# Head-pair attention reordered: two units transposed together, the next two scored, the first two mixed

## The chip, the cores and the metric

The kernel runs on one core of one Trainium2 chip. The metric is the device time of one launch in microseconds (us). A matmul or a transpose runs on TensorE (PE in the profile; PEld is its weight load), maxima and multiplications on VectorE (DVE), exponentials and copies on ScalarE (ACT), small elementwise work on GpSimd (POOL), and SyncE (SP) issues the weight DMAs.

## The reference

The whole network is five blocks on 512 latent and 256 context tokens: one hybrid layer (a recurrent branch beside a latent attention, "MLA"), then four layers of the kinds A, B, C, A. The change touches one kind of attention, which occurs three times: the MLA branch (8 heads, query and key width 96, value width 64), and the two A layers, layer 0 and layer 3 (16 query heads on 4 key/value heads, width 64). All in float32.

```
def softmax_attend(q, k, v):                       # MLA: 512 queries, 768 keys
    s = jnp.einsum('bqhd,bkhd->bhqk', q, k).astype(jnp.float32) * ATTN_SCALE
    p = jax.nn.softmax(s, axis=-1).astype(v.dtype)
    return jnp.einsum('bhqk,bkhd->bqhd', p, v)
...
mla_l = o * jax.nn.silu(g_mla)

def gqa_attention(q, k, v):                        # A layers
    ...
        logits = jnp.einsum("bqhgd,bkhd->bhgqk", qb, k).astype(jnp.float32) * scale
        p = jax.nn.softmax(logits, axis=-1).astype(v.dtype)
        return jnp.einsum("bhgqk,bkhd->bqhgd", p, v)
...
    o = gqa_attention(q, concat([kc, k]), concat([vc, v]))      # 512 queries, 768 keys
    oc = gqa_attention(qc, kc, vc) if need_ctx else None         # 256 queries, 256 keys
...
x = x + gt * ((o * jax.nn.silu(z)) @ w_out)
```

Layer 0 needs the context output `oc` too, layer 3 does not.

## The kernel before, in words

`pair_attention` (line 1193) is written once for all three places. A *unit* is one tile of 128 queries of a pair of heads (m = 0 and 1). MLA has 16 units (4 head pairs, 4 query tiles), layer 3 has 32, layer 0 has 32 and then 8 "joined" units, in which the two context tiles of a head pair stand side by side with 256 keys each. Four units (in the joined part one) make a *group*, whose result is gated and stored at once.

The steps of a unit, with their lines:

- scores (L1342 for the A layers, L1350 for MLA, L1317 joined): q times k into PSUM, 128 x 768 for each head. The two 64-row heads of an A layer run beside each other in the array.
- maximum (L1542; L1536 joined) on DVE, exponential with a running sum (L1477; L1491 joined) on ACT, into `prob`. In the profile an exponential is followed by a read of the accumulator, and it is this read that frees those who wait for the sum or the exponentials.
- turn (L1377; L1360 joined): 12 PE transposes of 128 x 128, in groups of four that fill one PSUM bank.
- evictions of the turned banks into `prob_t`: ACT (L1499) takes two of the three, DVE (L1560) one.
- mix (L1402; L1387 joined): `prob_t` times v into the OUT bank.
- DVE takes the reciprocal of the sums (L1554), POOL multiplies the gate tile z by it (L1614; L1610 joined), PE transposes z (L1424; L1416 joined), ACT copies it to `gate_t` (L1463, L1484), DVE multiplies OUT by it (L1571, L1567).

PE runs its instructions in the order in which the Python loops write them: turn unit i, mix unit i-1, score unit i+2. The PSUM places of the scores rotate: `place(i, m)` gives each head of a unit two of the six banks 0 to 5, so three heads' scores fit at a time, and the score of a unit waits until an older unit's exponentials are done. Transposes go into the banks that their own unit's scores leave free, and into bank 6 (TURN). Bank 7 is OUT.

Beside the attention, six steps of the next layer's modulation are done in MLA and in layer 0: `sum_rows` (L379) multiplies a weight chunk by a wide silu vector on PE, `mod_take` (L396, L398) adds the result on DVE, and at the end `mod_columns` (L389) turns it. They use what is free of the banks beside the scores. `mod_operands` (L362 to L365, DVE) prepares the silu vector.

In the A layers the attention starts inside the projection stage that precedes it: unit 0 is scored before the last pair of projections, and two gate multiplications of that stage (L1076) and two tanh copies (L850) are still to be done when unit 1 is scored.

Of the kernel before, what the change touches and what calls it, by code (L numbers as in the profile page):

```python
# [22 lines left out]
P = 128  # L23
# [1153 lines left out]
def pair_units(pairs):  # L1177

    units, groups = [], []
    for pair in pairs:
        if pair.get("joined"):
            units.append(dict(group=len(groups), col=0, last=True, joined=True, tiles=pair["tiles"]))
        else:
            for u, tile in enumerate(pair["tiles"]):
                units.append(dict(group=len(groups), col=u, last=u == len(pair["tiles"]) - 1, joined=False, **tile))
        groups.append(dict(dst=pair["dst"], last=len(units) - 1, z=[t["z"] for t in pair["tiles"]]))
    return units, groups  # L1190


def pair_attention(pr, local, pairs, next_mod, spare=None, entry=None):
# [7 lines left out]

    (scored, maxed, exped, filled, taken_a, taken_v, summed, scaled, mixed, finished, operands) = (
        pr.counter(s) for s in (
            "at_scored", "at_maxed", "at_exped", "at_turned", "at_moved_a", "at_moved_v", "at_chained", "at_weighted",
            "at_mixed", "at_stored", "mod_operands"))
    units, groups = pair_units(pairs)
    n = len(units)
    single = sum(not u["joined"] for u in units)
    TURN, OUT = pr.bank(6), pr.bank(7)
    gate_out, columns_out = pr.counter("sub_gated"), pr.counter("mod_copied")  # L1210
    mod_rows_at = {}
    for c in range(6 if next_mod else 0):
        at = (c + 1) * single // 7
        mod_rows_at[at - 1 if units[at]["last"] else at] = c
    late_gates = {i + 1: u["group"] for i, u in enumerate(units) if u["last"] and single < n and i >= single - 1}
    gates_at = {i + 2: u["group"] for i, u in enumerate(units) if u["last"] and i + 1 not in late_gates}
    rows_at = {i + 2: c for i, c in mod_rows_at.items()}
    row_steps = sorted(rows_at)
    mod_cols_at = max(mod_rows_at, default=-4) + 1

    def joined(i):
        return i < n and units[i]["joined"]

    def kts(i):
        return 4 if joined(i) else units[i]["keys"] // P

    def parts(i):

        return kts(i) // 2

    filled_at, taken_at, in_turn = {}, {}, []
    for i in range(n):
        for g in range(parts(i)):
            filled_at[i, g] = len(filled_at) + 1
            on_v = g == 1
            taken_at[i, g] = (taken_v if on_v else taken_a), sum(1 for _, h in taken_at if (h == 1) == on_v) + 1
            if g == 2 or parts(i) == 1:
                in_turn.append((i, g))

    def taken(i, g):  # L1240
        by, count = taken_at[i, g]
        return by.at(count)

    if spare is None:
        prob = local("prob", [P, 3, 2, TOK])
        prob_t = entry.free[:, 0:24 * P].rearrange("p (u x q) -> p u x q", u=2, x=12)
    else:
        flat = pr.h_t[:, :, :].rearrange("p k t -> p (k t)")
        prob = flat[:, 0:6 * TOK].rearrange("p (u m k) -> p u m k", u=3, m=2)
        prob_t = spare[:, 0:24 * P].rearrange("p (u x q) -> p u x q", u=2, x=12)  # L1250
# [8 lines left out]
    def place(i, m):  # L1259

        return 2 * ((2 * i + m) % 3)

    def score(i, m, a=0, b=TOK):

        return pr.bank(place(i, m), 2)[:, a:b]

    def joined_bank(i, m):

        return pr.bank(2 * ((2 * single - 3 + i - single) % 3) + m)

    def late_bank(i, gate):

        if i == single - 1:
            return TURN if gate else OUT
        return pr.bank(6 + (i - single) % 2)[:, CTX * gate:CTX * gate + CTX]  # L1280

    def late_gate_t(i):

        half = 0 if i == single - 1 else CTX * ((i - single) % 2)
        return gate_t[:, half:half + (SEQ if i == single - 1 else CTX)]

    def beside(i, m):

        return pr.bank(place(i, m), 2)[:, TOK:TOK + 256]

    def turn_bank(i, g):

        if joined(i):
            return joined_bank(i, g)
        return TURN if g == 2 or parts(i) == 1 else pr.bank(place(i, 1) + g)

    def gate_part(group, m):

        half = P * len(groups[group]["z"]) // 2
        return slice(half * m, half * m + half)

    def halves(x):
        return x.rearrange("p (x q) -> p x q", q=P)

    def tensor(pe, part):
        def joined_score(i):
            if i == single + 1:
                pe.wait_ge(*exped.at(2 * single - 1))  # L1310
            else:
                before = single - 2 if i == single else single - 1 if i == single + 2 else i - 3
                for g in range(2):
                    pe.wait_ge(*taken(before, g))
            for t, tile in enumerate(units[i]["tiles"]):
                for m in range(2):
                    last = pe.matmul(joined_bank(i, m)[:, CTX * t:CTX * t + CTX], tile["q"][m], tile["k"][m],  # L1317
                                     start=True, stop=True)
                    if t:
                        last.then_inc(*scored.tick())  # L1320

        def do_score(i):
            if joined(i):
                joined_score(i)
                return
# [3471 lines left out]
```

## Time and profile before

| | us |
|---|---|
| median of 3 runs | 2799.93 |
| lowest, highest run | 2796.51, 2800.12 |
| span of the profiled execution | 2795.5 |
| attention of MLA, first turn to last store | 99.2 |
| attention of layer 0 | 184.6 |
| attention of layer 3 | 145.6 |

The profile comes from a separate execution and gives its span, from the first to the last instruction; no whole time is listed for that execution. The median of the timed runs is 4.4 us above its span. The three attention parts are 429.4 us of the span. In the timeline a line is a run of like instructions of one engine: start, length to the end of the last one, and in brackets the idle time before it and who ended it. The length counts the pipeline of the last matmul, so the distance from one run's start to the next one's is the time that PE spent on it.

### The profile page before, as it was taken

The numbers are of one execution on the slowest core, as the hardware profiler recorded it, in microseconds if no ns is written. First come the engines' busy times: TensorE is split into PE (matmuls) and PEld (weight loads), VectorE is DVE, ScalarE is ACT, GpSimd is POOL, SyncE is SP. The second block draws the span as 40 slices with busy tenths as digits, with TensorE's granted clock in tenths as the row PEclk, the third lists the DMA queues.
The fourth block names the chain that finished last, engine by engine and source line by source line (L and its number), as shares of the span: only waits on it lengthen the run. The fifth ranks groups of instructions, "written<-read, shape, count | busy, mean of one in ns | idle before, by whom it ended". The sixth has DMA issues, their size and how long they took to land. (4 is left out here: it accounts for less than half of the span.)

```text
span 2795.5 us, 57678 instructions
## 1 busy us (share of the span) xinstructions
PE 2690.8 (96%) x23772; PEld 2129.5 (76%) x23772; DVE 1702.0 (61%) x3049; ACT 954.5 (34%) x2216; POOL 834.6 (30%) x1067
## 2 busy tenths in 40 slices
PE   7999999999999999999999999999999899999998
PEld 5978788785745887767688867777888676868886
DVE  5667876864426836564753357659833777576665
ACT  2022323224422136642121248321212675222661
POOL 3323333240024510012323115236531444254000
PEclk9999999999999999999999999999999999999999
DMA  6230100112432113303011161131011311212100
GB/s 242 92 128 20 44 18 3 49 36 69 144 114 80 61 48 134 107 1 106 33 60 61 61 223 30 52 112 61 31 61 61 136 62 61 94 59 81 77 2 31
DMA packets 108422, 205.88 MB, mean 74 GB/s; under 512 B 21923, under 2 KB 26162, under 8 KB 107648
## 3 DMA queue, kind: packets, MB, share of 16 engines
q1 hardware_dynamic: 107888, 201.30, 20.6%
q8 instruction: 189, 3.10, 0.5%
q0 software_dynamic: 272, 0.89, 0.1%
q14 instruction: 73, 0.60, 0.1%
HBM read 186.85 MB, written 15.54 MB: 72 GB/s over the span
## 5 line engine op out<-in xcount | busy, mean ns | idle before, releaser
L739 PE MATMUL psum<-weights,h_t 128*128 128x256 f32 x1488 | 355.5, 382 | 5.5 <-ACT early_work L828 5.5
L739 PEld LDWEIGHTS psum<-weights,h_t 128*128 128x128 f32 x1488 | 281.0, 191 | 45.4 <-ACT early_work L828 6.7
L1542 DVE TENSOR_REDUCE neg_max<-psum 128x1 f32<-128x768 f32 x160 | 152.3, 953 | 67.5 <-PE psum L1342 47.4
L739 PE MATMUL psum<-z_l,x_tiles 128*128 128x256 f32 x816 | 192.8, 379 | 0.5 <-POOL z_l L954 0.5
L739 PEld LDWEIGHTS psum<-z_l,x_tiles 128*128 128x128 f32 x816 | 155.0, 190 | 21.9 <-issue 0.9
L839 ACT ACTIVATE early_work<-psum 128x512 f32<-128x512 f32 (+1 forms) x80 | 45.0, 565 | 365.4 <-DVE psum L1112 250.0
L1112 DVE TENSOR_TENSOR psum<-psum,early_work 128x512 f32<-128x512 f32 x62 | 43.1, 695 | 144.5 <-PE psum L739 144.5
L1614 POOL TENSOR_TENSOR z_l<-z_l,inv_total 128x128 f32<-128x128 f32 x64 | 25.6, 400 | 346.8 <-DVE inv_total L1554 291.2
L1477 ACT ACTIVATE prob<-psum,neg_max 128x768 f32<-128x768 f32 x128 | 115.7, 904 | 14.1 <-DVE neg_max L1542 9.2
L739 PE MATMUL psum<-weights,x_tiles 128*128 128x256 f32 x496 | 117.2, 379 | 0.0
L1499 ACT ACTIVATE early_work<-psum 128x512 f32<-128x512 f32 x136 | 81.5, 599 | 96.4 <-PE psum L1377 96.4
L790 PE MATMUL psum<-weights,h_t 128*128 128x512 f32 x256 | 111.5, 593 | 1.2 <-PEq L240 1.2
L739 PE MATMUL psum<-z_l,h_t 128*128 128x256 f32 x408 | 97.5, 382 | 7.4 <-DVE early_work L1099 7.4
L739 PEld LDWEIGHTS psum<-weights,x_tiles 128*128 128x128 f32 x496 | 94.2, 190 | 12.8
L2824 POOL TENSOR_TENSOR x_tiles<-x_tiles,delta 128x512 f32<-128x512 f32 x36 | 47.8, 1329 | 182.2 <-DVE delta L2743 181.7
L1342 PE MATMUL psum<-k_l,q_l 64*128 64x256 f32 x768 | 100.2, 393 | 1.5 <-ACT prob L1477 1.5
L1377 PEld LDWEIGHTS psum<-eye,prob 128*128 128x128 f32 x768 | 82.7, 141 | 22.1 <-issue 14.6
L1377 PE MATMUL psum<-eye,prob 128*128 128x128 f32 x768 | 98.1, 277 | 0.8 <-ACT prob L1477 0.8
L1402 PE MATMUL psum<-early_work,v_l 128*64 128x128 f32 x1536 | 98.0, 277 | 0.0
L790 PEld LDWEIGHTS psum<-weights,h_t 128*128 128x128 f32 x256 | 48.0, 190 | 61.8 <-issue 61.8
L739 PEld LDWEIGHTS psum<-z_l,h_t 128*128 128x128 f32 x408 | 77.2, 191 | 21.1 <-DVE early_work L1099 10.6
L1402 PEld LDWEIGHTS psum<-early_work,v_l 128*64 128x64 f32 x1536 | 82.5, 137 | 10.7 <-ACT early_work L1499 8.1
(534 smaller groups left out, 6456.9 us busy)
## 6 DMA issues: line engine op xcount, KB each, us to landing
weights<-in_ada_w_dram SPq DMA_DIRECT2D x30, 2048.0 KB, 8.1
weights<-in_a_w_in_dram SPq DMA_DIRECT2D x10, 2048.0 KB, 8.4
weights<-in_b_w_in_dram SPq DMA_DIRECT2D x8, 2048.0 KB, 7.8
weights<-in_c_w_in_dram SPq DMA_DIRECT2D x8, 2048.0 KB, 7.9
weights<-in_w_in_dram SPq DMA_DIRECT2D x6, 2048.0 KB, 8.8
x_aside<-x_tiles SPq DMA_DIRECT2D x24, 512.0 KB, 2.7
x_tiles<-x_aside SPq DMA_DIRECT2D x4, 3072.0 KB, 15.8
weights<-in_a_w_out_dram SPq DMA_DIRECT2D x4, 2048.0 KB, 7.9
```

The costliest lines, as they stand in the source:

```text
L739: last = pe.matmul(dst, lhs[:, k, :], rhs[k // 2][:, k % 2, :], start=k == 0, stop=k == KH - 1)
L790: last = pe.matmul(ps(i), pr.h_t[:, k, P * t:P * t + P], w[:, k, :], start=(k == 0), stop=(k == KT - 1))
L839: act.activation(square[:, j % 2, 0:w], ps(i)[:, 0:w], ACT.Square).then_inc(*squared.tick())
L1112: dve.tensor_tensor(left_ps, left_ps, terms[:, 0:2, :], ALU.add).then_inc(*projected.tick())
L1342: last = pe.matmul(score(i, m, a, a + 256), units[i]["q"][m], units[i]["k"][m][:, a:a + 256], start=True, stop=True)
L1377: last = pe.transpose(turn_bank(i, g)[:, P * x:P * x + P], prob[:, i % 3, m, P * kt:P * kt + P], pr.eye[:, :])
L1402: last = pe.matmul(OUT[64 * m:64 * m + 64, P * col:P * col + P], units[i]["v"][m][kt], prob_t[:, i % 2, 2 * kt + m, :], start=(kt == 0), s ...
L1477: act.activation(prob[:, i % 3, m, 0:keys], score(i, m, 0, keys), ACT.Exp, bias=neg_max[:, i % 4, m:m + 1], accum_out=total[:, i % 4, m:m ...
L1499: act.activation(prob_t[:, i % 2, 4 * g:4 * g + 4, :], halves(turn_bank(i, g)), ACT.Copy)\
L1542: last = dve.tensor_reduce(neg_max[:, i % 4, m:m + 1], score(i, m, 0, keys), AX, ALU.max, negate=True)
L1614: pool.tensor_tensor(z, z, wide(inv[:, i % 4, 0:2], 2, 64), ALU.mult).then_inc(*scaled.tick())
L2824: pool.tensor_tensor(pr.X[:, tiles[i], cols], pr.X[:, tiles[i], cols], delta[:, u % 2, :], ALU.add)\
```

## The change

`pair_attention` is rewritten around pairs of units (p, with units 2p and 2p+1); the arithmetic stays. In words:

- PE order: turn both units of pair p (24 transposes), score both units of pair p+1, then the row sums if there are any, then mix both units of pair p.
- PSUM: banks 0 to 2 belong to head 0, banks 3 to 5 to head 1. Each three banks hold the scores of the two units end to end (2 x 768 columns). The transposes of the pair go into the same banks, in three steps of eight: step e fills bank e (evicted by ACT) and bank 3+e (evicted by DVE), so each of the two has 1.5 evictions per unit. The scores of the next pair wait for those evictions step by step. Bank 6 (SIDE) serves gates, row sums and modulation columns; bank 7 is OUT.
- Step 0 waits for the exponentials of unit 2p, step 1 for those of unit 2p+1. The maximum of the second unit waits for the exponential of the first unit's same head, since the two share a bank.
- The gate transposes of a group stand before the last step of turns of its last pair, and wait there for POOL's multiplication (`scaled`). One ACT copy of 512 columns takes them.
- Joined units are also done in pairs: 4 pairs, four context tiles per group.
- Row sums after the scores of pairs 2, 4, ..., 12 (layer 0) or 0 to 5 (MLA), in one 512-column piece.
- At the start of an A layer unit 0 and unit 1 are scored where they were; pair 1 is scored after both are turned.

```
         if part == "first":
             if entry:
                 entry.scores(pe)
-            do_score(0)
+                score_alone(0)
+            else:
+                score_pair(0)
             return
         if entry:
             entry.second_place(pe)
-        for i in range(-1, n + 1):
-            if 0 <= i < n:
-                do_turn(i)
...
-            if i >= 1:
-                do_mix(i - 1)
...
-            if i + 2 < n or i + 2 in gates_at:
-                do_score(i + 2)
+            pe.wait_ge(*exped.at(2))
+            score_alone(1)
+        for p in range(n_pairs):
+            turn_pair(p)
+            if p + 1 < n_pairs:
+                score_pair(p + 1)
+            if p == 0 and entry:
+                entry.all_places(pe)
+            if p in rows_at:
+                sum_rows(p)
+            do_mix(2 * p)
+            do_mix(2 * p + 1)
+            if p == columns_at:
...
+                mod_columns(pe, SIDE[:, 0:48], mod_rows, pick).then_inc(*columns_done.tick())
```
```
+        def score_pair(p):
+            c, d = 2 * p, 2 * p + 1
...
+            if p:
+                wait_taken(p - 1, 0)
+            if by_rows:
+                for a in (0, 256):
                     for m in range(2):
+                        score(c, m, a, a + 256)
...
+            if p:
+                wait_taken(p - 1, 1)
             for m in range(2):
+                score(c, m, 512, 768)
+            for m in range(2):
+                score(d, m, 0, 256).then_inc(*scored.tick())
+            if p:
+                wait_taken(p - 1, 2)
+            if by_rows:
+                for m in range(2):
+                    score(d, m, 256, 512)
+                for m in range(2):
+                    score(d, m, 512, 768).then_inc(*scored.tick())
...
+        def turn_pair(p):
+            a, b = 2 * p, 2 * p + 1
...
+            def wait_gates():
+                pe.wait_ge(*scaled.at(b + 1))
+                if gates_at[p]:
+                    pe.wait_ge(*gate_out.at(gates_at[p]))
+                side_free(p)
+
+            pe.wait_ge(*exped.at(2 * a + 2))
+            for x, block in enumerate(blocks):
+                e, half, at = x // 8, x // 4 % 2, P * (x % 4)
+                if x == 8:
+                    pe.wait_ge(*exped.at(2 * b + 2))
+                if x == len(blocks) - 8 and zs:
+                    wait_gates()
+                    for y, z in enumerate(zs):
+                        pe.transpose(SIDE[:, P * y:P * y + P], z, pr.eye[:, :])
+                last = pe.transpose(half_place(half)[:, SEQ * e + at:SEQ * e + at + P], block, pr.eye[:, :])
+                if x % 8 == 7:
+                    last.then_inc(*filled.tick())
```
ScalarE and VectorE, their loops:
```
+        for p in range(n_pairs):                      # scalar
...
+            for e in range(steps(p)):
+                take_step(p, e)
+            if p in gates_at:
+                take_gate(gates_at[p])
+            if p + 1 < n_pairs:
+                for i in (2 * p + 2, 2 * p + 3):
+                    for m in range(2):
+                        do_exp(i, m)
...
+            if i % 2:                                 # vector, do_max
+                dve.wait_ge(*exped.at(2 * i + m - 1))
...
+        for p in range(n_pairs):                      # vector
+            if p - 1 in gates_at:
+                finish(gates_at[p - 1])
+            if p:
+                do_inverse(2 * p)
+                do_inverse(2 * p + 1)
+            for e in range(steps(p)):
+                take_step(p, e)
+            if p + 1 < n_pairs:
+                for i in (2 * p + 2, 2 * p + 3):
+                    for m in range(2):
+                        do_max(i, m)
+            if p == 0:
+                if beside_second:
+                    beside_second()
+                if next_mod:
+                    mod_operands(pr, dve, silu_w, pick, 1, operands, 6)
+                do_inverse(0)
+                do_inverse(1)
+            if p in rows_at:
+                c = rows_at[p]
+                dve.wait_ge(*rows_done.at(c + 1))
+                mod_take(dve, mod_rows[:, :], SIDE, c, rows_taken.at(max(c, 1))).then_inc(*rows_taken.tick())
+        finish(len(groups) - 1)
```

## Rows read from the trace of the kernel before

**Rows 1.** The page: span of the profiled execution.
```profile
span 2795.5 us, 57678 instructions
```
**Rows 2.** By stretch: busy PE, PEld, DVE, ACT, POOL; granted clock; DMA.
```profile
677.49:776.71 99.22, 97.66 (x905) 70.73 (x903) 47.11 (x79) 47.79 (x101) 6.01 (x15) 1.00 0.37 128
1045.00:1229.56 184.56, 182.22 (x1954) 142.82 (x1952) 112.71 (x190) 119.84 (x286) 18.89 (x48) 1.00 0.27 98
2591.55:2737.18 145.63, 143.36 (x1546) 118.39 (x1544) 90.37 (x135) 97.50 (x206) 12.77 (x32) 1.00 0.09 38
```
**Rows 3.** Timeline, layer 3: start, length, engine, line, [idle before].
```profile
2657.52 1.57 PE L1342 MATMUL psum<-k_l,q_l 64*128 64x256 f32 x12
2658.34 0.17 DVE L1554 RECIPROCAL inv_total<-total 128x2 f32<-128x2 f32 x1 [1.06 <-ACT prob L1477]
2658.59 0.40 POOL L1614 TENSOR_TENSOR z_l<-z_l,inv_total 128x128 f32<-128x128 f32 x1 [4.02 <-DVE inv_total L1554]
2659.02 1.53 PE L1377 MATMUL psum<-eye,prob 128*128 128x128 f32 x12
2660.15 0.69 DVE L1560 COPY early_work<-psum 128x512 f32<-128x512 f32 x1
2660.48 1.53 PE L1402 MATMUL psum<-early_work,v_l 128*64 128x128 f32 x24
2661.94 0.66 PE L1424 MATMUL psum<-eye,z_l 128*128 128x128 f32 x4
2662.53 1.57 PE L1342 MATMUL psum<-k_l,q_l 64*128 64x256 f32 x12
```
**Rows 4.** Timeline, start of layer 3: maxima and exponentials back to back.
```profile
2583.67 1.81 DVE L1542 TENSOR_REDUCE neg_max<-psum 128x1 f32<-128x768 f32 x2
2584.65 0.90 ACT L1477 ACTIVATE prob<-psum,neg_max 128x768 f32<-128x768 f32 x1 [4.46 <-DVE neg_max L1542]
2585.40 1.28 DVE L1076 SCALAR_TENSOR_TENSOR z_l<-tanh_z,z_l 128x512 f32<-128x512 f32 x2
2585.54 0.89 ACT L1477 ACTIVATE prob<-psum,neg_max 128x768 f32<-128x768 f32 x1
2586.32 0.20 ACT L1477 ACTIVATION_READ_ACCUMULATOR prob<-psum,neg_max 128x1 f32 x1
```
**Rows 5.** Timeline, layer 3, unit 1 after the first turn begins.
```profile
2591.65 0.96 DVE L1542 TENSOR_REDUCE neg_max<-psum 128x1 f32<-128x768 f32 x1 [0.27 <-PE psum L1342]
```
**Rows 6.** Timeline, layer 3's last turn, for which PE waits.
```profile
2731.16 0.19 ACT L1477 ACTIVATION_READ_ACCUMULATOR prob<-psum,neg_max 128x1 f32 x1
2731.40 1.53 PE L1377 MATMUL psum<-eye,prob 128*128 128x128 f32 x12 [0.77 <-ACT prob L1477]
```
**Rows 7.** Timeline, layer 0, a row sum and the scores behind it.
```profile
1065.62 1.93 PE L379 MATMUL psum<-weights,silu_wide 128*32 128x256 f32 x32
1067.48 1.57 PE L1342 MATMUL psum<-k_l,q_l 64*128 64x256 f32 x12
```
**Rows 8.** Timeline, layer 0's joined units.
```profile
1214.31 1.14 PE L1317 MATMUL psum<-k_l,q_l 64*128 64x256 f32 x8
1215.48 1.29 DVE L1536 TENSOR_REDUCE neg_max<-psum 128x2 f32<-128x512 f32 x2 [1.04 <-PE psum L1317]
1216.62 1.08 PE L1387 MATMUL psum<-early_work,v_l 128*64 128x256 f32 x8
1216.93 0.76 POOL L1610 TENSOR_TENSOR z_l<-z_l,inv_total 128x128 f32<-128x128 f32 x2 [2.56 <-DVE inv_total L1554]
```
**Rows 9.** Timeline, MLA: the turns of two neighbouring units.
```profile
682.36 1.48 PE L1377 MATMUL psum<-eye,h_t 128*128 128x128 f32 x12
687.91 1.48 PE L1377 MATMUL psum<-eye,h_t 128*128 128x128 f32 x12
```
**Rows 10.** By stretch, outside the attention (columns as in rows 2).
```profile
541.50:543.70 2.20, 1.56 (x50) 1.42 (x50) 2.17 (x4) 0.60 (x1) 0.00 (x0) 1.00 0.44 102
543.00:550.00 7.00, 5.13 (x116) 4.99 (x116) 4.88 (x8) 0.00 (x0) 2.44 (x3) 0.76 0.38 141
```

More of the change, by code:

```diff
@@ L1205, in pair_attention @@
             "at_mixed", "at_stored", "mod_operands"))
+    gate_out, columns_out = pr.counter("sub_gated"), pr.counter("mod_copied")
+    rows_done, rows_taken, columns_done = pr.counter("mod_multiplied"), pr.counter("mod_taken"), pr.counter("mod_turned")
     units, groups = pair_units(pairs)
[L1207 to L1238, printed above, removed]
@@ new lines, in joined, with half_place, score_at, blocks_of @@
+    def joined(i):
+        return units[i]["joined"]
+    def half_place(m):
+        return pr.bank(3 * m, 3)
+    def score_at(i, m):
+        if entry and i == 0 and m:
+            return pr.bank(2, 2)[:, 0:TOK]
+        size = SEQ if joined(i) else TOK
+        return half_place(m)[:, size * (i % 2):size * (i % 2) + size]
+    def blocks_of(i):
+        if joined(i):
+            return [(m, CTX * t + P * kt) for m in range(2) for kt in range(2) for t in range(2)]
+        return [(m, P * kt) for kt in range(units[i]["keys"] // P) for m in range(2)]
@@ new lines, in score_alone, with side_free @@
+        def score_alone(i):
+            for a in (0, 256, 512):
+                for m in range(2):
+                    last = score(i, m, a, a + 256)
+                    if a == 512:
+                        last.then_inc(*scored.tick())
+        def side_free(p):
+            before = [c for at, c in rows_at.items() if at < p]
+            if before:
+                pe.wait_ge(*rows_taken.at(max(before) + 1))
+            if 0 <= columns_at < p:
+                pe.wait_ge(*columns_out.at(1))
@@ new lines, in do_mix @@
+        def do_mix(i):
+            unit = units[i]
+            wait_taken(i // 2, steps(i // 2) - 1 if i % 2 else steps(i // 2) - 2)
+            if unit["at"] == 0 and unit["group"]:
+                pe.wait_ge(*finished.at(unit["group"]))
+            if joined(i):
+                for kt in range(2):
+                    for m in range(2):
+                        x = turned_at(i, 4 * m + 2 * kt)
+                        last = pe.matmul(OUT[64 * m:64 * m + 64, unit["at"]:unit["at"] + CTX], unit["tiles"][0]["v"][m][kt],
+                                         prob_t[:, x:x + 2, :].rearrange("p x q -> p (x q)"), start=(kt == 0), stop=(kt == 1))
+                last.then_inc(*mixed.tick())
+                return
+            kts = unit["keys"] // P
+            for kt in range(kts):
@@ L1385, in joined_mix @@
                 for m in range(2):
[L1386 to L1388 removed]
+                    last = pe.matmul(OUT[64 * m:64 * m + 64, unit["at"]:unit["at"] + P], unit["v"][m][kt],
+                                     prob_t[:, turned_at(i, 2 * kt + m), :], start=(kt == 0), stop=(kt == kts - 1))
@@ L1506, in scalar @@
             return
[L1507 to L1521 removed]
+        do_exp(1, 0)
```

380 lines of the change are left out of this document (116 added, 264 removed).

## The prediction

> **What bounds the kernel now.** I read the busy time of the three attention stretches first. PE is busy for 97.66 of 99.22, 182.22 of 184.56 and 143.36 of 145.63 us, DVE and ACT for 47 to 67% of it, at a full clock (1.00, the level of 2.4 GHz) [rows 2]. So PE's instruction stream sets the time, and every other engine has slack. The timeline then gives the period. In layer 3 a unit is scores at 2657.52, turns at 2659.02, mix at 2660.48, next kind at 2661.94: 1.50 + 1.46 + 1.46 = 4.42 us, with DVE's maximum, evictions and POOL's scaling beside it. A gate adds 0.59 (2661.94 to 2662.53) every fourth unit [rows 3]. Two pairs with one gate are 18.27 us, or 9.13 per pair.
>
> What part of a run is work and what is switching? Four transposes are 0.66 long and twelve 1.53 [rows 3]: 0.109 per transpose. Eight score records are 1.14 long and twelve 1.57 [rows 8, 3]: 0.217 per two heads' records, which run beside each other. Mix records come two at a time as well, twelve steps, again 0.109 each, since the run of 24 has the length of twelve transposes [rows 3]. So 1.46 for twelve steps of 0.109 = 1.31 leaves 0.15 for the change of kind; scores leave 1.50 - 1.30 = 0.20.
>
> **The change part by part.** The matmuls, transposes and columns are the same. What changes is the number of changes of kind and the waits.
>
> *PE's own work per pair of units* (A layers): turns 1.46 + 12 x 0.109 = 2.77, scores 1.50 + 6 x 0.217 = 2.80, mixes 2.77: 8.34 instead of 8.84. Half of the switching is gone, 0.50 us per pair. A gate inside the turns costs 4 x 0.109 = 0.44 instead of 0.59.
>
> *The new chain.* Before, three heads' scores are kept in rotation and the turns of a unit find their exponentials done two units ahead. Now six banks hold just one pair: nothing of pair p+1 can be scored before pair p is turned, and its exponentials must be done before its own turns. In that time PE has only the mixes. From S, the first score of a pair: the first unit's scores are signalled by the 8th step, 1.57 + 2 x 0.217 = 2.00. Two maxima back to back take 1.81 [rows 4] and one takes 0.96 [rows 5]; an exponential takes 0.98 to the end of its read (2585.54 to 2586.52), and the next may start 0.89 after it [rows 4]; a released engine starts about 0.04 later (PE at 2731.40 after a read that ended at 2731.35: 0.05) [rows 6].
>   - maxima c0, c1: 2.03 to 3.84, c0 done at 2.98. Exponentials c0: 3.02 to 4.00, c1: 3.91 to 4.90. The first unit is ready at 4.90.
>   - maximum d0 waits for exponential c0, 4.04 to 5.00; d1 for c1, 4.94 to 5.89. Exponentials d0: 5.04, d1: 5.93 to 6.92. The second unit is ready at 6.92, and PE may go on at 6.97.
>   - PE meanwhile: scores to 2.80, mixes to 5.57, the first eight transposes (ready at 4.90, no wait) to 6.45. Then it waits 0.52 until 6.97. The other 16 take 1.46 + 0.44 = 1.90: 8.87.
>
> So a pair takes 8.87, with its share of the gate (0.22) 9.09, against 9.13: the 0.50 won by fewer changes goes into a stall of 0.52 at the ninth transpose. The evictions do not prolong it: step 1 is filled at about 8.0, step 2 at 8.9, each eviction is 0.69 at most [rows 3], and the scores that need step 2 come 1.8 after the next S. That ACT has one half eviction less per unit is worth nothing, since ACT is not late anywhere.
>
> *Row sums* (L379) cost 1.86 each on PE (1065.62 to 1067.48) [rows 7]. In layer 0 they now stand ahead of the mixes, so they push the first transposes from 5.57 to 7.43, behind the point 6.97: of 1.86 only 1.86 - 0.52 = 1.34 lengthen the pair. Six of them: -3.1 us; the modulation columns the same way: -0.5.
>
> *Layer 3 in full.* First turn at 2591.55 [rows 2]. Unit 1: maximum at 2591.65, the second ends at 2593.46 (1.81), its exponential at 2594.5 [rows 4, 5]; PE's eight transposes are done at 2592.5 and it waits until 2594.57, then 1.90: S of pair 1 is 4.92 after the start. Then 15 x 8.87 = 133.05 and 8 gates x 0.44 = 3.5. Once, at pair 1, the gate transposes wait for POOL: DVE does the two held-over gate products (1.28 [rows 4]) after the maxima, and only then the four reciprocals, and POOL needs 4 x 0.40 [rows 3] behind them: PE is held about 1.2. Then mixes 1.53 + 1.31 = 2.84 and the last product 0.73 (0.69 for a 512-column DVE operation, as an eviction, and the release). Sum 146.2 against 145.63 [rows 2]: +0.6.
>
> *Layer 0.* The same 4.92 + 133.05 + 3.5, POOL's wait 1.6 (the modulation operands stand in DVE's way as well), row sums 6 x 1.34 = 8.0, columns 0.5: 151.6. Joined pairs: scores signalled at 1.13 and 1.99, maxima 1.29 for two [rows 8], eight exponentials of 256 columns; I take 0.46 for each, the rate at which half the width would go (0.89 / 2), and 0.1 for the last read, which puts the first unit at 3.8 and the second at 5.65. PE has scores and mixes until 3.8 and eight transposes until 4.8. The gate now stands at the ninth transpose and waits for DVE's reciprocal and POOL's two multiplications (0.76) [rows 8] behind the last exponential: 5.65 + 0.17 for the reciprocal [rows 3] + 0.76 + three releases of 0.05 = 6.74. Then 12 transposes, 1.46: 8.20 per joined pair, three times, 8.6 the first time (POOL is later there, behind a longer mix), and 2.7 for the end: 35.9. Together 187.5 against 184.56 [rows 2]: +2.9. This is the dearest piece, a wait of some 2 us four times.
>
> *MLA.* The unit is 5.55 (682.36 to 687.91) [rows 9], since the 96-row scores of the two heads do not run side by side. PE's stream per pair is then about 10.8, longer than the chain (second unit ready near 8.2), so there is no stall and the switching is won, with this array shape some 0.3 per pair: 7 x -0.3 = -2.2. Against it the first row sum, now behind pair 0, waits for the silu operands, which DVE makes after pair 1's four maxima: about +2.3. Row sums gain nothing here. Sum +0.1.
>
> Total: +0.6 + 2.9 + 0.1 = +3.6. The profiled span would be 2795.5 + 3.6 = 2799.1 [rows 1]; with the 4.4 us by which the median stands above the span, **2803.5 us**.
>
> Bounds. The stall per pair is the one number that counts, 24 to 31 times. From below: all of it gone, 0.52 x 30 = -16 us. From above: if releases and the paired DVE and ACT work each run a tenth late (seven links), 0.4 more per pair, +12. The joined wait lies between nothing (-8) and a whole unit's chain, 3.8 more once per pair (+15); I take the value worked out, whose links all have rows.
>
> **A rule against the change.** In the nearest place of this trace a stretch of transposes alone (541.5 to 543.7) still has the granted clock 1.00, and in the 7 us after it, with PE busy for 5.13, the mean falls to 0.76 (part of it at 1.2 GHz) [rows 10]. TensorE: Matmul & The Clock Gate of the Trainium skill (Part 4, PE-mode transpose) says that a transpose does not count as PE work for the clock. If that held, 24 transposes with a stall among them would be the emptiest stretches of each pair. The trace does not decide it: the turns before never stood longer than 1.5 us together.
>
> **The rivals.**
> - *Clock falls* (slower). Turns and stall together last 3.3 to 3.7 us in a pair and 4.4 in a joined pair, where before no turn outlasted 1.53. If the clock drops to 1.2 GHz in the joined pairs alone, PE's 4 us of work per pair double: 4 x 1 to 2 us, 2810. If in every pair, PE's 2.8 us of mixes or turns behind the drop take twice as long, 30 x 1.5 = 45: 2850. For it: rows 10. Against: PE is still busy for 94% of a pair. It decides from the point at which turns plus stall are too quiet for the gate.
> - *Longer chain* (slower). Each of the seven links a little later, 0.15 to 0.4 per pair: 2808 to 2816. For it: ACT and DVE now read PSUM at the same time in every link. Against: maxima and exponentials already run beside each other before, at 0.96 and 0.90.
> - *PE stays the bound* (faster). The second unit's exponentials are ready at the ninth transpose after all, by 0.5 us earlier somewhere in the chain; then a pair is 8.34 + 0.22 and the kernel 2803.5 - 16 = 2788. For it: a stall of 0.52 is a small difference of two long sums. Against: each link has its row.
> - *Nothing else*: that the weights come late for the moved row sums. They are at least 11 us apart in MLA and 18 in layer 0; PE never waited for a chunk before.
>
> **How the numbers follow.** A difference of 0.2% (5.6 us) is about what a measurement of this kernel can tell. Around the median of 2799.9 that is 2794.3 to 2805.5. Forecast 2803.5, own range 2797 to 2809: 0.50, of it 0.01 under 2794.3 and 0.12 over 2805.5. Longer chain 0.20 and clock 0.10, all of it slower. PE bound 0.20, of it 0.04 within the bound, for a stall only partly gone. So faster 0.17, same 0.37 + 0.04 = 0.41, slower 0.12 + 0.30 = 0.42. Likeliest single case is still the forecast; the range, 2787 to 2817, reaches over PE bound and the longer chain and leaves out most of the clock case and the tails.
>
> **What would show it.** In layer 3 a pair every 8.9 us and 9.3 with a gate; PE idle about 0.5 in each, in front of the ninth transpose, released by the exponential (ACT); the PE busy sum of the stretch lower by about 7 us and its length unchanged. In pairs with a row sum no idle time. In MLA no idle time but one of 2 us before the first row sum, released by DVE. In the joined part a gap of 1.9 us released by POOL. The step on the chain is wrong if pairs of layer 3 are under 8.6 or over 9.2 without a gate; the forecast as a whole fails if the granted clock leaves 1.00 inside the attention.

## The result, and the profile after

| | us |
|---|---|
| changed kernel, median of 20 runs (lowest to highest) | 2803.45 (2798.49 to 2818.65) |
| kernel before on the same chip, median of 20 runs | 2797.83 (2794.41 to 2805.0) |
| ratio, 95% interval | 1.0028 [1.0017, 1.004] |
| span of the profiled execution, after / before | 2799.4 / 2795.5 |

The medians differ by 5.6 us, the ratio makes 7.8 us (4.8 to 11.2) of it. The changed kernel is slower, since the interval lies above 1. Whether it is slower by more than the 0.2% that the prediction took as its bound is not settled, since the interval reaches below 1.002. The upper runs of the changed kernel pull the ratio further than the medians.

First the stretches, from the first turn to the last store of MLA, layer 0 and layer 3, as in [rows 2]: busy PE, PEld, DVE, ACT, POOL, then the granted clock.

```profile
676.39:776.85 100.46, 96.20 (x808) 68.93 (x808) 52.06 (x83) 44.51 (x89) 6.10 (x16) 0.98 0.36 127
1045.70:1233.52 187.82, 173.94 (x1858) 142.21 (x1856) 121.75 (x197) 112.14 (x259) 18.65 (x48) 1.00 0.27 96
2593.86:2741.11 147.25, 137.81 (x1546) 120.02 (x1544) 98.31 (x152) 89.93 (x182) 12.64 (x32) 1.00 0.09 37
```

PE's busy time fell by 8.3 us in layer 0 and 5.6 us in layer 3, and both stretches grew all the same: the kernel does less on PE and waits more. There PE was busy for 98 to 99% of the time before and is for 93 to 94% now.

The timeline of one pair of layer 3 shows the wait (start, length, engine, line, what; in brackets the idle time before it and who ended it).

```profile
2636.70 2.86 PE L1291 MATMUL psum<-k_l,q_l 64*128 64x256 f32 x24
2638.73 1.82 DVE L1494 TENSOR_REDUCE neg_max<-psum 128x1 f32<-128x768 f32 x2 [1.23 <-PE psum L1291]
2639.49 2.84 PE L1389 MATMUL psum<-early_work,v_l 128*64 128x128 f32 x48
2639.72 0.90 ACT L1447 ACTIVATE prob<-psum,neg_max 128x768 f32<-128x768 f32 x1 [2.32 <-DVE neg_max L1494]
2640.82 1.84 DVE L1494 TENSOR_REDUCE neg_max<-psum 128x1 f32<-128x768 f32 x2 [0.26 <-ACT prob L1447]
2641.81 0.90 ACT L1447 ACTIVATE prob<-psum,neg_max 128x768 f32<-128x768 f32 x1 [0.21 <-DVE neg_max L1494]
2642.26 1.09 PE L1369 MATMUL psum<-eye,prob 128*128 128x128 f32 x8
2643.49 0.19 ACT L1447 ACTIVATION_READ_ACCUMULATOR prob<-psum,neg_max 128x1 f32 x1
2643.74 1.09 PE L1369 MATMUL psum<-eye,prob 128*128 128x128 f32 x8 [0.38 <-ACT prob L1447]
2644.66 0.60 PE L1368 MATMUL psum<-eye,z_l 128*128 128x128 f32 x4
2645.10 1.04 PE L1369 MATMUL psum<-eye,prob 128*128 128x128 f32 x8
```

Read it as a relay, in which each engine waits for the one before it: two maxima (2638.73), the first exponential (2639.72), the maxima of the second unit (2640.82), its exponential (2641.81), the read of the last sum (2643.49 to 2643.68), and 0.06 later the ninth transpose. Between the eighth transpose and the ninth PE starts nothing for 0.54 us, the 0.109 of the eighth not counted. The bracket says 0.38, since the pipeline of the last transpose counts as busy. The next pair starts at 2646.07: 9.37 us with a gate, 8.93 without (8.87 and 9.31 were worked out).

In layer 0's joined pairs a second wait stands ahead of the gate's transposes:

```profile
1206.10 2.08 PE L1290 MATMUL psum<-k_l,q_l 64*128 64x256 f32 x16
1209.99 1.09 PE L1369 MATMUL psum<-eye,prob 128*128 128x128 f32 x8
1211.78 0.18 DVE L1502 RECIPROCAL inv_total<-total 128x4 f32<-128x4 f32 x1 [0.90 <-ACT prob L1442]
1212.03 0.76 POOL L1560 TENSOR_TENSOR z_l<-z_l,inv_total 128x128 f32<-128x128 f32 x2 [0.32 <-DVE inv_total L1502]
1212.89 0.63 PE L1368 MATMUL psum<-eye,z_l 128*128 128x128 f32 x4 [1.81 <-issue]
1214.32 0.92 PE L1290 MATMUL psum<-k_l,q_l 64*128 64x256 f32 x6
```

PE is idle for 1.81 us; the bracket names "issue", but POOL's product ends at 1212.79, 0.1 before. A joined pair takes 8.22 us (8.20 worked out).

One thing stands in the stretches that was put under the rivals: MLA has a mean clock of 0.98. The windows around it (columns as before):

```profile
676.00:678.40 2.40, 1.10 (x8) 0.86 (x8) 2.09 (x3) 2.19 (x7) 0.00 (x0) 1.00 0.00 0
678.40:681.80 3.40, 3.32 (x16) 3.32 (x17) 0.69 (x1) 1.11 (x3) 0.00 (x0) 0.50 0.00 0
681.80:684.00 2.20, 2.20 (x8) 1.22 (x7) 0.69 (x1) 0.60 (x1) 0.00 (x0) 1.00 0.00 0
```

In the first, PE is busy for 1.10 of 2.40 us: it waits for the first two units' exponentials. Then 3.4 us run at 0.50 (1.2 GHz), in which PE is busy for 3.32 and gets through 16 instructions, at 0.21 us each instead of 0.109. The trace of before has no such stretch inside the attention.

### The profile page after: what moved, and what is told of

The parts are those of the page before. It is cut to its first block and busy times, and to the rows that moved or that the text cites. A ratio compares the mean times of both kernels' runs of the same rounds, so it can differ in the third digit from the quotient of the medians.

```text
span 2799.4 us, 57392 instructions
## 1 busy us (share of the span) xinstructions
PE 2676.5 (96%) x23580; PEld 2127.6 (76%) x23580; DVE 1720.4 (61%) x3073; ACT 935.2 (33%) x2153; POOL 831.8 (30%) x1067
## 5 line engine op out<-in xcount | busy, mean ns | idle before, releaser
L1494 DVE TENSOR_REDUCE neg_max<-psum 128x1 f32<-128x768 f32 x160 | 146.5, 954 | 67.7 <-PE psum L1291 57.4
L1369 PE MATMUL psum<-eye,prob 128*128 128x128 f32 x832 | 107.5, 277 | 12.9 <-ACT prob L1447 12.9
L1369 PEld LDWEIGHTS psum<-eye,prob 128*128 128x128 f32 x832 | 90.6, 141 | 25.7 <-ACT prob L1447 18.7
L1509 DVE COPY early_work<-psum 128x512 f32<-128x512 f32 x104 | 71.6, 689 | 44.2 <-PE psum L1369 43.9
L1291 PE MATMUL psum<-k_l,q_l 64*128 64x256 f32 x768 | 92.1, 385 | 0.0
L1389 PE MATMUL psum<-early_work,v_l 128*64 128x128 f32 x1536 | 90.9, 275 | 0.0
```

Of the source, the lines that this page charges most:

```text
L1291: return pe.matmul(score_at(i, m)[:, a:b], unit["q"][m], unit["k"][m][:, a:b], start=True, stop=True)
L1369: last = pe.transpose(half_place(half)[:, SEQ * e + at:SEQ * e + at + P], block, pr.eye[:, :])
L1389: last = pe.matmul(OUT[64 * m:64 * m + 64, unit["at"]:unit["at"] + P], unit["v"][m][kt], prob_t[:, turned_at(i, 2 * kt + m), :], start=(kt ...
L1494: dve.tensor_reduce(neg_max[:, i % 4, m:m + 1], score_at(i, m), AX, ALU.max, negate=True)\
L1509: dve.tensor_copy(dst, src).then_inc(*taken_v.tick())
```

## The experiments

### Is the chain the bound in a pair?

```
-  dve.tensor_reduce(neg_max[...], score_at(i, m), AX, ALU.max, negate=True)
+  dve.tensor_reduce(neg_max[...], score_at(i, m)[:, 0:256], AX, ALU.max, negate=True)
-  act.activation(prob[...], score_at(i, m), ACT.Exp, bias=neg_max[...], ...)
+  act.activation(prob[...], score_at(i, m), ACT.Exp, bias=pr.ones[:, 0:1], scale=2.0 ** -6, ...)
```

> The changed kernel, in which the maxima of the non-joined units read only the first 256 of 768 columns and the exponential takes a constant bias and a scale of 1/64, so the output is not the reference's; every wait, copy and matmul stays. Theory (the chain maximum, exponential, maximum, exponential through six banks sets the pair, and PE stalls 0.6 us at its ninth transpose): a maximum falls from 0.95 to about 0.41 us, the second unit is ready some 0.8 us earlier, the stall in layers 0 and 3 disappears, and a pair of layer 3 without a gate falls from 8.93 to about 8.35 us: 15 pairs of layer 3 and 8 of layer 0, 13 to 15 us in all, 2787 to 2791 us (ratio to before 0.996 to 0.998); MLA's pairs (12.56 with a row sum) unchanged. Rival (PE's own pace, bank traffic or issue sets the pair and the gap at the ninth transpose is only where it shows): pairs stay at 8.9, the time stays at 2803.

Measured: 2786.17 us, 0.8 below the range expected; ratio 0.9952 [0.9935, 0.9969]. The maxima of all units but the joined ones read 256 of 768 columns, and the exponentials use a constant in their place; PE's work is the same. Layer 3 fell from 147.25 to 137.54 us. PE in one of its pairs with a gate, and the start of the next pair:

```profile
2646.05 2.86 PE L1291 MATMUL psum<-k_l,q_l 64*128 64x256 f32 x24
2648.84 2.84 PE L1389 MATMUL psum<-early_work,v_l 128*64 128x128 f32 x48
2651.61 1.97 PE L1369 MATMUL psum<-eye,prob 128*128 128x128 f32 x16
2653.41 0.60 PE L1368 MATMUL psum<-eye,z_l 128*128 128x128 f32 x4
2653.85 1.04 PE L1369 MATMUL psum<-eye,prob 128*128 128x128 f32 x8
2654.82 2.86 PE L1291 MATMUL psum<-k_l,q_l 64*128 64x256 f32 x24
```

There is no bracket left: 8.77 us with a gate. The pair before it, without one, starts at 2637.72 and takes 8.33, PE's own work (8.34 was worked out). The reordering does win its 0.50 us a pair in changes of kind; the chain of maxima and exponentials takes it away.

The second run asks the same from the other side. It leaves the chain as it is and puts work of no use into the stall of layer 3:

```
+                if x == 8 and p > 1 and not next_mod:
+                    wait_gates_out(p - 1)
+                    for _ in range(4 if p % 2 else 8):
+                        pe.transpose(SIDE[:, 0:P], pr.eye[:, :], pr.eye[:, :])
                 if x == 8:
                     pe.wait_ge(*exped.at(2 * b + 2))
```

> The changed kernel with useless transposes (0.109 us each) right in front of the ninth transpose of layer 3's pairs 2 to 15: eight (0.87 us) in even pairs, four (0.44 us) in odd ones. If the chain maximum, exponential, maximum, exponential sets the pair and PE has some 0.54 us of stall there, the odd pairs stay as they are (9.37 us with their gate) and the even ones grow from 8.93 by 0.87 - 0.54 = 0.33, so that layer 3's attention goes from 147.25 to 149.6 us and the kernel to 2805.8 us. Rival, that PE is the bound and the idle time shown is only the pipeline's: every pair grows by what was added, 7 x 0.87 + 7 x 0.44 = 9.2 us, 156.4 and 2812.6 us.

Measured: layer 3 took 149.24 us, 2.0 more, where 2.4 were expected of the chain and 9.2 of a bound PE; the kernel 2806.89 us, ratio 1.0039 [1.0024, 1.0054]. PE in an even pair's turns and in the odd pair behind it (L1366 is what was added):

```profile
2636.72 1.09 PE L1373 MATMUL psum<-eye,prob 128*128 128x128 f32 x8
2637.65 1.04 PE L1366 MATMUL psum<-eye 128*128 128x128 f32 x8
2638.52 1.91 PE L1373 MATMUL psum<-eye,prob 128*128 128x128 f32 x16
2640.36 2.86 PE L1291 MATMUL psum<-k_l,q_l 64*128 64x256 f32 x24
2643.16 2.84 PE L1393 MATMUL psum<-early_work,v_l 128*64 128x128 f32 x48
2645.93 1.09 PE L1373 MATMUL psum<-eye,prob 128*128 128x128 f32 x8
2646.86 0.60 PE L1366 MATMUL psum<-eye 128*128 128x128 f32 x4
2647.40 1.09 PE L1373 MATMUL psum<-eye,prob 128*128 128x128 f32 x8
2649.73 2.86 PE L1291 MATMUL psum<-k_l,q_l 64*128 64x256 f32 x24
```

2640.36 to 2649.73 is 9.37, the same as without the four transposes: 0.44 us of work went into the stall for nothing. An even pair grew from 8.93 to 9.20, so of its 0.87 us the stall took 0.60. The first run says the same, 8.93 - 8.33 = 0.60. Two runs, one that shortens the chain and one that fills the stall, agree on its size.

### The gate's place

```
+        def turn_gate(p):                       # PE: behind score_pair(p + 1), no longer ahead of the last turns
+            pe.wait_ge(*scaled.at(2 * p + 2))
+            ...
+            for y, z in enumerate(groups[gates_at[p]]["z"]):
+                last = pe.transpose(SIDE[:, P * y:P * y + P], z, pr.eye[:, :])
...
+        def take_gate(group):                   # DVE: behind the maxima of pair p + 1, no longer on ACT
+            ...
+            dve.tensor_copy(gate_t[:, :], SIDE).then_inc(*gate_out.tick())
```

> The changed kernel with the gate transposes of the two A layers taken out of the turns and put behind the scores of the next pair, ahead of the mixes, where POOL's scaling is long done; DVE instead of ACT copies the gate, after its four maxima. Theory (stall has room, POOL's wait is on the path): the gate's 0.44 us falls into the stall, a pair with a gate of layer 3 goes from 9.37 to about 8.95 us (8 pairs in each of the layers 0 and 3: -7), the waits of 1.0 and 1.6 us for POOL at pair 1 vanish (-2.6), a joined pair goes from 8.22 to about 6.85 us (4 pairs: -5.5): together about -15, 2788 us, ratio to before 0.9965. Rival (joined pairs and gates are held by the exponentials alone, POOL being late costs nothing of its own, or the gate copy on DVE delays the evictions by as much): joined pairs stay over 7.8 us and the time within 4 us of 2803.

Measured: 2793.36 us, ratio 0.998 [0.9967, 0.9994]: faster than before, and by the medians 10.1 us under the changed kernel (by the two ratios 13.4), where 15 and a time of 2788 were expected. Layer 0 went from 187.82 to 180.38, layer 3 from 147.25 to 143.27 us. Layer 0 has a stretch of 3.4 us at half clock here, 4.2 us after its first turn. By a later trace without one (194.03 from first score to last product, against 203.10) the two layers are 13.0 us shorter at full clock. PE in the joined part (L1380 is the gate):

```profile
1201.89 2.01 PE L1291 MATMUL psum<-k_l,q_l 64*128 64x256 f32 x16
1203.83 0.66 PE L1380 MATMUL psum<-eye,z_l 128*128 128x128 f32 x4
1204.42 1.95 PE L1392 MATMUL psum<-early_work,v_l 128*64 128x256 f32 x16
1206.30 1.09 PE L1370 MATMUL psum<-eye,prob 128*128 128x128 f32 x8
1207.57 1.09 PE L1370 MATMUL psum<-eye,prob 128*128 128x128 f32 x8 [0.18 <-ACT prob L1454]
1208.59 2.08 PE L1291 MATMUL psum<-k_l,q_l 64*128 64x256 f32 x16
```

6.70 us in place of 8.22 (6.85 was expected): the wait for POOL was on the path, and not only the exponentials. In layer 3 the gate is free as well: behind the scores it makes PE later at the ninth transpose by 0.58, where 0.54 were idle, and a pair with a gate takes 8.94 (2635.56 to 2644.50) beside 8.93 without. Ahead of the last turns it stood behind the stall, and its 0.44 us were paid in full, eight times.

### MLA's operands

```
                 take_step(p, e)
+            if p == 0 and next_mod and not entry:
+                mod_operands(pr, dve, silu_w, pick, 1, operands, 6)
             if p + 1 < n_pairs:                 # the maxima of pair 1
```

> The changed kernel with one thing moved: in MLA, DVE makes the silu operands of the row sums before the four maxima of pair 1, not after. Theory (PE's first row sum waits for DVE): the gap of 2.6 us ahead of the first row sum goes, the row sum runs directly behind the scores (0.52 us after the last one's start), MLA is 2 to 2.6 us shorter, some 0.4 us of it may come back as a later maximum; 2801 us, ratio to before 1.002. Rival (the row sum waits for its weights, whose transfer was queued at the same time): the gap stays, released by a DMA.

In the changed kernel the first row sum waits behind four maxima:

```profile
689.41 0.17 DVE L365 COPY silu_wide<-silu_c 128x16 f32<-128x16 f32 x1
689.74 1.92 PE L379 MATMUL psum<-weights,silu_wide 128*32 128x512 f32 x16 [2.53 <-DVE silu_wide L365]
```

With the edit this idle time is gone and MLA takes 96.25 us from the first turn. A second trace of the changed kernel, with no half-clock stretch in MLA, has 98.85, so the wait is worth 2.6 us (2.3 was worked out). The kernel: 2800.72 us where 2801 was expected, ratio 1.0001 [0.9988, 1.0015], 2.7 us less than the changed kernel's median. This trace has 6.8 us at half clock from just before MLA's first score, so its time from the first score, 105.52 us, can't be compared.

### Sharing the evictions, by itself

The kernel before, with the third eviction of every odd unit on DVE:

```
+    def dve_takes(i, g):
+        return g == 1 or (g == 2 and i % 2 == 1)
```

> The kernel before, with only the eviction split of the change: of every odd unit's third eviction DVE takes what ACT took, so each engine has 1.5 per unit. Theory (PE sets the unit, 4.42 us, and no eviction is late): layer 3 stays at 145.6 us within 0.5, ratio to before 1.000. Rival (ACT's load of two evictions is what the change relieves): layer 3 shorter by more than 1 us. Other rival (DVE's copy stands ahead of its second maximum and delays the exponential): longer by 0.3 us per odd unit, 10 us over the two A layers.

Measured: 2801.91 us, ratio 1.0009 [0.9997, 1.0021], no difference that can be told. Layer 3 keeps its 145.63 us to the digit, with 7.9 us less on ACT and 9.6 more on DVE:

```profile
2590.99:2736.62 145.63, 143.36 (x1546) 118.40 (x1544) 99.94 (x151) 89.57 (x190) 12.77 (x32) 1.00 0.09 37
```

PE's and POOL's columns are those of [rows 2]. So the shared eviction alone is worth nothing in a kernel that PE bounds. Layer 0 took 1.3 us more, with a new PE gap of 1.11 ahead of the modulation columns, released by DVE.

### Both moves together

The gate's move and the operands' move in one kernel.

> The changed kernel with both earlier moves together: in the A layers the gate transposes stand behind the next pair's scores and DVE copies them, and in MLA the modulation operands are made ahead of pair 1's maxima. If the two act in different stages and add up, the gate's move keeps its 10 us (2793.4 us measured) and MLA's idle time of 2.5 us before the first row sum goes as well: 2791 us (2789 to 2793), with MLA's attention, first score to end, at 104 us or less instead of 106.7, joined pairs at 6.7 us and layer 0 at 180.4 us. Rival, that MLA's gap was covered by something else late in the same place (the tiles of pair 1 come later by what the operands took): 2793.4 us, no gain over the gate's move alone.

Measured: 2787.98 us (2784.94 to 2793.89), ratio 0.9968 [0.9956, 0.9979]: 10.2 us under the kernel before by the medians (2798.19 in those rounds), 9.0 by the ratio, 1 us under the range expected. No full version here is faster beyond the noise. The two gains add up by stage: at full clock MLA keeps the 2.6 us and the A layers their 13.0. Its trace has half-clock stretches at two of the three starts:

```profile
2590.00:2592.10 2.10, 0.17 (x2) 0.14 (x2) 1.47 (x3) 2.06 (x5) 0.00 (x0) 1.00 1.05 407
2592.10:2595.50 3.40, 3.40 (x18) 3.07 (x18) 0.69 (x1) 0.90 (x2) 0.00 (x0) 0.50 1.09 424
```

### Does the silence of PE cost clock?

```
+        def keep_busy(out, times):
+            for _ in range(times):
+                pe.matmul(out, pr.eye[:, :], pr.eye[:, :], start=True, stop=True)
...
+            if p == 0 and not entry:
+                keep_busy(SIDE[:, 0:P], 3)           # MLA, ahead of the first transpose; 4 ahead of the ninth
             pe.wait_ge(*exped.at(2 * a + 2))
+            if p == 0 and entry:
+                keep_busy(half_place(0)[:, 0:P], 8)  # A layers
...
+                    keep_busy(SIDE[:, 0:P], 7)       # joined pairs, only in the first of these runs
```

> The changed kernel with matmuls of no use (128x128 by 128x128, some 0.22 us each, results overwritten) in its long stalls: three and four in front of MLA's first and ninth transpose, eight in front of the A layers' first transpose, seven in front of POOL's wait in each joined pair; every other step as it was. Both theories: PE is waiting there, so the added 6 to 7 us of PE time lengthen nothing, and joined pairs stay at 8.22 us. If it is the silence of PE in these stalls that lets the granted clock fall to 1.2 GHz inside the attention (3.4 us at half clock, which cost some 1.5 us where it hit MLA's start), no halved stretch is found in the three attention parts, the median is 1 to 2 us lower, 2802, and the runs above 2809 us (7 of 20 of the changed kernel) become rare. Rival, that the halved stretches in the attention are chance and the upper runs have another source: 2803.5 us and a third of the runs above 2809. Third, that the fillers are not covered: 2810 us.

> The both-moves version with the same useless matmuls in the stalls that are left, those at the start of the three attention parts (three and four in MLA, eight in each A layer). If the silence there costs clock: 1 us less than the both-moves version, 2790 us, and no halved stretch in the attention. If it doesn't: equal to it, 2791 us. If the eight matmuls are not covered by the A layers' start stall of 2.2 us: 0.5 to 2 us more, 2793 us.

> The changed kernel once more, for a second trace of it. So far every stretch at half clock inside the attention of the changed kernel and of its variants began within 1.3 us of the end of a PE stall of over 0.85 us. If the stalls are what lets the clock fall, this trace has zero to three such stretches, each at a listed stall. If they fall by chance, a stretch may as well stand in the middle of layer 3, where there are 14 pairs without a long stall.

> The both-moves version with useless matmuls in the starting stalls, once more. Stall theory: again no stretch at half clock in the three attention parts, and the parts last 102.5, 194.0 and 158.6 us from first score to last product. Chance: one or two, as in most traces of the unfilled kernels, and 1.6 us more for each.

> The same version, but what fills the starting stalls are useless transposes in place of matmuls: six and eight in MLA, sixteen in each A layer, 0.109 us each. If any work of PE keeps the clock up, no stretch at half clock in the attention and the lengths of the version filled with matmuls (102.5, 194.0, 158.6 us). The Trainium skill (TensorE: Matmul & The Clock Gate, Part 4, PE-mode transpose) says that transposes don't count as work for the clock; if that holds, the starts are as silent as in the unfilled both-moves version, which had a stretch at half clock at two of its three starts, and these lengths are 1.6 us more where one falls.

> The version filled with transposes once more, since one trace without a fall of the clock says little. Expected as for the run before: no half-clock stretch at the three starts if transposes count, one or two if they don't.

By the medians nothing was won. The changed kernel with filled stalls took 2807.84 us (ratio 1.0024 [1.0013, 1.0036]), not the 2802 expected, and 3 of its 11 runs lie above 2809. The medians come from different rounds, and by the ratio it equals the changed kernel (1.0028). Part of the difference of the medians was my filler: in the joined pairs it starts behind the exponentials and ends later than POOL, 8.77 us a pair in place of 8.22, 1.7 us in all; some 3 us stay unexplained. The filled both-moves version took 2788.65 us (ratio 0.9962 [0.9947, 0.9977]), the same as unfilled, and under all three of its expectations (2790 to 2793). The last four were single runs, taken for their traces: 2804.84 for the changed kernel, 2790.97 for the both-moves version filled with matmuls, 2790.59 and 2785.02 filled with transposes, beside 2798.38 for the kernel before.

The traces speak more clearly. The second one of the changed kernel, three stalls and what follows each:

```profile
1059.00:1060.80 1.80, 0.54 (x5) 0.55 (x6) 0.95 (x2) 0.56 (x1) 1.20 (x4) 0.99 0.05 14
1060.80:1064.20 3.40, 3.40 (x18) 2.81 (x17) 0.69 (x1) 1.08 (x2) 0.00 (x0) 0.50 0.00 0
...
1230.00:1231.40 1.40, 0.24 (x2) 0.27 (x3) 0.77 (x2) 0.50 (x2) 0.76 (x2) 1.00 0.00 0
1231.40:1234.80 3.40, 3.40 (x18) 2.68 (x18) 0.69 (x1) 1.05 (x2) 0.00 (x0) 0.50 0.00 0
2598.00:2600.20 2.20, 1.35 (x12) 1.35 (x13) 0.57 (x2) 1.50 (x4) 0.00 (x0) 0.99 1.05 405
2600.20:2603.60 3.40, 3.40 (x18) 2.62 (x18) 1.17 (x2) 0.98 (x2) 0.00 (x0) 0.50 1.21 491
```

These are POOL's wait in pair 1, a joined pair and layer 3's start. Over eight traces (two of the changed kernel, six of variants that keep long stalls) 14 stretches at half clock lie in the attention, and each begins between 0.6 us before and 1.3 us after the end of a stall of 1.26 us or more (from one start of PE to the next). These traces have 57 stalls over 1.2 us there. A fifteenth stretch, the one ahead of MLA's first score with the operands moved, begins 0.6 us before the end of a gap of 1.32. None lies among layer 3's pairs with only the 0.54 us stall, which are most of the time. The kernel before and its variant with shared evictions, whose gaps between the first score and the last mix of a part are at most 1.16 us, have none in two traces. The both-moves version with filled starts has no stall over 1.2 us left there, and none of these stretches in four traces (two filled with matmuls, two with transposes). The starts of one filled with transposes:

```profile
676.50:700.00 23.50, 23.23 (x163) 16.35 (x164) 12.58 (x22) 10.58 (x22) 1.51 (x4) 1.00 0.34 123
1032.34:1060.00 27.66, 27.10 (x205) 23.18 (x205) 15.78 (x24) 13.59 (x28) 0.00 (x0) 1.00 0.47 187
2572.03:2600.00 27.97, 27.41 (x208) 23.48 (x208) 16.11 (x27) 13.60 (x28) 0.40 (x2) 1.00 0.49 187
```

All four have, from first score to last product, 102.46, 194.0 and 158.5 to 158.6 us. Unfilled, the both-moves version has 104.10, 194.03 and 160.16: 1.6 us more exactly where a stretch fell. So the stalls do let the clock fall, not every time, at 1.6 us each. At zero to three per execution this hides in the medians, since stretches elsewhere in the kernel move single runs by more.

Whether transposes fill as well as matmuls is less sure. The six starts filled with transposes had no fall of the clock, and in each of the four of the A layers 40 transposes ran within 4.9 us at clock 1.00. But of the 21 unfilled starts only 7 were followed by a stretch, so six without one would come by chance about one time in eleven (an estimate from that share). TensorE: Matmul & The Clock Gate of the Trainium skill (Part 4, PE-mode transpose) says that transposes do not count as work for the clock; these two traces lean against it for float32 transposes and don't refute it.

## Why the prediction was right or wrong

**The number.** 2803.5 was forecast and 2803.45 measured, closer than the reasoning deserves. Two errors cancel. The 4.4 us between span and median is no property of an execution: the changed kernel's profiled execution took 2801.16 us with a span of 2799.4, 1.8 above it. In all the runs the time is 1.7 to 1.9 above the span. So the base was 2797.3, which is also what 20 later runs gave (2797.83); the three runs shown lay 2 us high. And the change costs 5.6 to 7.8 us, not 3.6. That the two nearly cancel is luck.

**Where the time went, by stage,** from first score to last product at full clock:

| | before | after | predicted change | measured |
|---|---|---|---|---|
| MLA | 105.51 | 105.06 (second trace) | +0.1 | -0.45 |
| layer 0 | 199.83 | 203.10 | +2.9 | +3.3 |
| layer 3 | 160.91 | 162.53 | +0.6 | +1.6 |
| sum | | | +3.6 | +4.4 |

The missing 1.2 to 3.4 us goes with the clock. Among runs with the same mean clock, 0.995, the changed kernel's four have a median of 2802.1 and 16 later runs of the kernel before one of 2798.0: 4.0 us, about what the stages give. The rest is that the 20 runs had a lower mean clock, 0.9928 against 0.9947 in 56 later runs of the kernel before, where 0.001 goes with some 2 us. The attention's part of it is one stretch of 1.6 us in the first trace and three in the second. That the change causes all of it isn't shown. Of the 20 runs, 7 took 2808.9 us or more, and these have the lowest mean clocks (0.992 or less, the others 0.993 and more); none of them was traced, so where they lost it stays open.

**Step by step.**
- *PE's own work, 8.34 per pair*: right (8.33 with short maxima).
- *The chain, ninth transpose at 6.97 after S, stall 0.52*: right in mechanism and place; measured 7.04 (2636.70 to 2643.74) and 0.54. The pair is 0.06 longer than worked out, nearly all in one link: the second unit's maximum starts 1.10 after the first exponential (2639.72 to 2640.82), not 1.02. Times 15 this is 0.9 us, nearly all of layer 3's error.
- *The start of 4.92*: exact (2593.86 to 2598.78). *POOL's wait at pair 1*: 1.2 and 1.6 worked out; pair 1 takes 10.71 in layer 3 and 10.91 in layer 0, 1.34 and 1.54 more than a later pair with a gate.
- *Row sums in the stall*: right. In a layer 0 pair with one, the transposes run on without a bracket, and the pair with its gate takes 10.62, PE's own 8.34 + 1.85 + 0.44. That is 1.25 more than without the row sum; 1.34 was worked out.
- *Joined pairs, 8.20*: 8.22, and moving the gate (6.70) showed that it was the gate's wait.
- *MLA*: the wait for the operands 2.3, measured 2.6; the switching won was undersized. Without the wait MLA is at 96.25 against 99.22, 3.0 us less rather than 2.2.
- *Evictions worth nothing*: right, by the variant of the kernel before.
- *PE busy sum of layer 3 lower by 7*: 5.6. Part of each stall counts as busy (0.54 is idle, the bracket has 0.38); that this is the whole difference isn't shown.
- *Rival, the clock*: given 0.10 in all, as a fall in every joined pair or in every pair. It is real but rarer: after single long stalls, 1.6 us at a time, also at the starts and at POOL's wait, which I had not listed. My own sentence that the forecast fails if the clock leaves 1.00 inside the attention was met; what failed is the completeness of the sum, not its terms. The rows that I set beside the Trainium skill's rule on transposes could not test it: the run from 541.5 to 543.7 turns its tiles with plain matmuls by the identity (L3543), not with transposes.

What I left on the table was the other side of my own working. I called the joined wait the dearest piece and took the gate's place as given. The same numbers (0.52 us idle, a gate of 0.44 to 0.59 placed behind the idle time instead of in front of it) say that the gate's move makes the change a gain.

## What to carry to other kernels

When work on the bounding engine is merged into longer runs, write down its new dependency cycle before counting the saving: six banks that hold just one pair turn free-running units into a relay, and the relay's length (8.93) replaced the engine's work (8.34). Put side work of that engine (gates, row sums) ahead of its stall, where it is free, and not behind it; here that and the earlier operands turned +5.6 us into -10.2 us by the medians. Before a new wait on an engine is accepted, look for what else is queued on the releaser, as the operands behind four maxima were.

## What the runs showed of the hardware

- The granted clock fell to 1.2 GHz at 14 of 57 PE stalls of 1.2 to 3.1 us in eight traces, and at none of the 0.54 us stalls of layer 3's pairs. The halved stretches in the rows are 3.4 us long, PE is busy through most of each, and one costs 1.6 us.
- Useless matmuls or transposes in a stall cost nothing where they end before the releaser (filled starts: 194.0 us with and without) and 0.55 us a time where they end after it.
- Merging two runs of each kind into one saves PE 0.50 us per pair of units (8.84 to 8.33), seen once the chain is short enough: with maxima a third as wide layer 3 went from 147.25 to 137.54 us with PE's work unchanged.
